# Gate and up products of a two-layer encoder: rounded tokens and their rests side by side as one 512-column product, halves added on GpSimd

## What is computed

```python
h = rmsnorm(x, norm_ffn)
ff = jax.nn.silu(h @ w_gate) * (h @ w_up)
return x + ff @ w_down
```

## Time and profile before

| | |
|---|---|
| median of 3 runs | 1264.53 us (1263.86 to 1264.61) |
| the profiled execution | 1263.36 us |
| its span on the core | 1261.6 us, granted TensorE clock 0.999 of full |
| PE | 1236.0 us busy (98% of the span) |
| DVE | 701.7 us (56%) |
| ACT | 683.6 us (54%) |
| POOL | 672.6 us (53%) |
| chain that ended last | PE 86%, DVE 6%, ACT 4%, issue 2%, POOL 1%, DMA 1% |

### The profile page before, as it was taken

The page is one execution under the profiler, slowest core; times in us unless marked ns, Lnnn a source line. Parts: engine busy times, 40 slices in busy tenths (PEclk is TensorE's granted clock), DMA queues, the critical chain, the costliest instruction groups (busy, mean ns, idle before and its releaser), DMA issues.

```text
span 1261.6 us, 23375 instructions
## 1 busy us (share of the span) xinstructions
PE 1236.0 (98%) x9232; PEld 1072.2 (85%) x9232; DVE 701.7 (56%) x1110; ACT 683.6 (54%) x1342; POOL 672.6 (53%) x484
## 2 busy tenths in 40 slices
PE   7999999999999999999999999999999999999997
PEld 6767787879999999888877777788899999998886
DVE  6845576677776777300058465665877767750003
ACT  6756655448665555432256766554576555553233
POOL 3745752557465354666626776338364433346662
PEclk9999999999999999999999999999999999999999
DMA  6211211232222222332222212214122233323232
GB/s 249 84 52 52 68 51 68 73 145 90 101 102 101 101 101 84 118 100 97 89 72 78 68 51 68 69 51 150 51 85 101 101 108 116 113 85 111 91 99 84
DMA packets 31501, 115.99 MB, mean 92 GB/s; under 512 B 3488, under 2 KB 3872, under 8 KB 31008
## 3 DMA queue, kind: packets, MB, share of 16 engines
q1 hardware_dynamic: 31392, 114.49, 26.5%
HBM read 112.37 MB, written 2.10 MB: 91 GB/s over the span
## 4 chain that ended last, share of the span: by engine, by line
PE 86%; DVE 6%; ACT 4%; issue 2%; POOL 1%; DMA 1%; POOLq 0%; SPq 0%; ACTq 0%; DVEq 0%
PE ps L1998 11%; PE ps L2001 10%; PE ps L2000 10%; PE ps L1855 6%; PE ps L1857 6%; PE ps L1877 6%; PE ps L1874 6%; PE ps L1875 6%; PE ps L1856 6%; PE ps L2157 2%; PE ps L2143 2%; PE ps L1871 2%; PE ps L1866 2%; PE ps L1868 2%; POOL w_lo L1175 1%
## 5 line engine op out<-in xcount | busy, mean ns | idle before, releaser
L1175 POOL TENSOR_TENSOR w_lo<-w_raw,w_hi 128x1024 fp32r<-128x1024 f32 x108 | 265.2, 2457 | 295.7 <-ACT w_hi L686 238.8
L686 ACT ACTIVATE w_hi<-w_raw 128x1024 fp32r<-128x1024 f32 x108 | 114.0, 1056 | 186.4 <-PE ps L1877 170.8
L1998 PE MATMUL ps<-h_hi,w_hi 128*128 128x256 f32 x672 | 191.0, 284 | 0.0
L2000 PE MATMUL ps<-h_lo,w_hi 128*128 128x256 f32 x672 | 190.1, 283 | 0.0
L2001 PE MATMUL ps<-h_hi,w_lo 128*128 128x256 f32 x672 | 190.1, 283 | 0.0
L1855 PE MATMUL ps<-h_hi,w_hi 128*128 128x512 f32 (+1 forms) x392 | 166.3, 424 | 1.4 <-DVE g L1604 0.7
L1998 PE MATMUL ps<-sum_hi,w_hi 128*128 128x256 f32 x528 | 150.2, 284 | 3.6 <-DVE silu L1406 2.2
L1857 PE MATMUL ps<-h_hi,w_lo 128*128 128x512 f32 (+1 forms) x392 | 152.0, 388 | 0.0
L1856 PE MATMUL ps<-h_lo,w_hi 128*128 128x512 f32 (+1 forms) x392 | 151.2, 386 | 0.0
L2000 PE MATMUL ps<-sum_lo,w_hi 128*128 128x256 f32 x528 | 149.4, 283 | 0.0
L2001 PE MATMUL ps<-sum_hi,w_lo 128*128 128x256 f32 x528 | 149.3, 283 | 0.0
(11 more groups left out here) (277 smaller groups left out, 2823.7 us busy)
## 6 DMA issues: line engine op xcount, KB each, us to landing
w_raw<-in_units SPq DMA_DIRECT2D x110, 512.0 KB, 3.5
u<-in_pairs SPq DMA_DIRECT2D x44, 512.0 KB, 4.3
w_raw<-in_pairs SPq DMA_DIRECT2D x40, 512.0 KB, 4.3
gain<-in_gain SPq DMA_DIRECT2D x5, 512.0 KB, 4.3
par<-in_par SPq DMA_DIRECT2D x2, 1214.5 KB, 6.2
x<-in_x SPq DMA_DIRECT2D x4, 512.0 KB, 7.1
spec<-in_pairs SPq DMA_DIRECT2D x4, 512.0 KB, 5.1
out_y<-x SPq DMA_DIRECT2D x3, 512.0 KB, 2.6
```

What stands on the lines that cost most here:

```text
L686: nc.scalar.activation(w_tile(g, 0), w_raw[:, g % RAW], ACT.Copy).then_inc(s_hi, 1)
L1175: nc.gpsimd.tensor_tensor(w_tile(g, 1), w_raw[:, g % RAW], w_tile(g, 0).bitcast(F32), ALU.subtract).then_inc(s_lo, 1)
L1998: nc.tensor.matmul(out, hi[:, cols], factor[m][0][:, k], start=start and k == 0, stop=False, skip_group_check=True)
L2000: nc.tensor.matmul(out, hi[:, cols], factor[m][1][:, k], start=False, stop=False, skip_group_check=True)
```

## The change

For pairs 4 to 21 (`WIDE` = 4) the two matmuls of `m1`, `m6`, `m7` and `m4` that share the rounded weights become one: the rounded tokens and their rests are stored in one tensor (`h_parts`, `sum_parts`), so that one matmul of 512 columns reads both and writes both halves of the bank. The third matmul (rest of the weights) adds to the first half. The bank then holds two partial sums, so:

- ACT copies 512 columns instead of 256 in `copy_m1`, `copy_u2`, `copy_u3`, and a new `copy_gate` copies the bank after `m4` to SBUF;
- POOL adds the halves of each copy (`fold`, 128x256, in place), four a pair, at places of its order that the excerpt below shows;
- `m2` moves to the spare bank's first half, and the filters' and the net's outputs of the first layer's stage to its second half;
- `silu_second(p)` runs on the folded gate in SBUF, behind `copy_u2(p+1)`, and `hidden_second(p)` after the rest of m4(p+1), with both inputs in SBUF;
- `m6` waits for `copy_m1`, not for `gate_first`;
- the filters' `window_sums` on POOL go: a second set of sine values with one half's sign turned lets the filter matmuls over all 128 rows make sum and difference. POOL keeps one addition to a row (`skip_row`), twice.

```diff
+WIDE = 4
+def wide(m, p):
+    return p >= WIDE and m in ("m1", "m6", "m7", "m4")
...
             def copy_u2(L, p):
                 act.wait_ge(prod_done.sem, prod_done.at(L, NUMBER["m6", p] + 1))
+                if p >= WIDE:
+                    act.wait_ge(up1.sem, up1.at(L, p - 1))
...
+                    nc.scalar.activation(wide_u2(p), both(p), ACT.Copy).then_inc(u2c.sem, 1)
+                    return
...
+            def copy_gate(L, p):
+                act.wait_ge(prod_done.sem, prod_done.at(L, NUMBER["m4", p] + 1))
+                act.wait_ge(hid2d.sem, hid2d.at(L, p - 1))
+                nc.scalar.activation(wide_gate(p), both(p), ACT.Copy).then_inc(g2c.sem, 1)
+
             def silu_second(L, p):
+                if p >= WIDE:
+                    act.wait_ge(g2f.sem, g2f.at(L, p - WIDE + 1))
+                    nc.scalar.activation(wide_gate(p)[:, FIRST], wide_gate(p)[:, FIRST], ACT.Silu).then_inc(silu2.sem, 1)
+                    return
...
                     copy_u2(L, p)
+                    if p - 1 >= WIDE:
+                        silu_second(L, p - 1)
                     hi_item(L, NUMBER["m4", p])
...
-                    silu_second(L, p)
+                    if p >= WIDE:
+                        copy_gate(L, p)
+                    else:
+                        silu_second(L, p)
...
+            def fold(L, p, t, copied, at, done):
+
+                pool.wait_ge(copied.sem, copied.at(L, at))
+                nc.gpsimd.tensor_tensor(t[:, FIRST], t[:, FIRST], t[:, SECOND], ALU.add).then_inc(done.sem, 1)
...
                 for j in range(12, N_ITEMS):
+                    m, p = ITEMS[j]
+                    if m == "m3" and WIDE <= p < LAST:
+                        fold_u2(L, p)
                     if not rest_on_vector(j):
                         lo_item(L, j)
-                    m, p = ITEMS[j]
+                    if m == "m2" and p - 2 >= WIDE:
+                        fold_gate(L, p - 2)
+                    if m == "m3" and WIDE <= p < LAST:
+                        fold_u3(L, p)
+                    if m == "m3" and WIDE <= p + 1 < FT:
+                        fold_m1(L, p + 1)
+                    if m == "m3" and p == LAST - 1:
+                        fold_gate(L, p)
...
+                fold_u2(L, LAST)
                 lo_unit(L * UNITS + U_DOWN)
+                fold_u3(L, LAST)
+                fold_gate(L, LAST)
                 lo_unit(L * UNITS + U_DOWN + 1)
...
             def up_second(L, p):
 
                 v.wait_ge(prod_done.sem, prod_done.at(L, NUMBER["m5", p] + 1))
+                if p >= WIDE:
+                    v.wait_ge(u3f.sem, u3f.at(L, p - WIDE + 1))
+                    to = u3w[p % 2][:, FIRST]
+                    nc.vector.tensor_tensor(to, fourth(p), to, ALU.add).then_inc(up2d.sem, 1)
+                    return
...
                     lo_item(L, NUMBER["m4", p])
+                    if p - 1 >= WIDE:
+                        hidden_second(L, p - 1)
...
                 for k in range(KT // 2):
                     cols = slice(P * k, P * k + P)
-                    nc.tensor.matmul(out, hi[:, cols], factor[m][0][:, k], start=start and k == 0, stop=False,
-                                     skip_group_check=True)
-                    nc.tensor.matmul(out, hi[:, cols], factor[m][1][:, k], start=False, stop=False, skip_group_check=True)
-                    last = nc.tensor.matmul(out, lo[:, cols], factor[m][0][:, k], start=False, stop=k == KT // 2 - 1,
+                    if wide(m, p):
+                        nc.tensor.matmul(both(p).rearrange("p (v t) -> p v t", v=2), hi[:, cols], factor[m][:, :, k],
+                                         start=start and k == 0, stop=False, skip_group_check=True)
+                    else:
+                        nc.tensor.matmul(out, hi[:, cols], factor[m][:, 0, k], start=start and k == 0, stop=False,
+                                         skip_group_check=True)
+                        nc.tensor.matmul(out, hi[:, cols], factor[m][:, 1, k], start=False, stop=False,
+                                         skip_group_check=True)
+                    last = nc.tensor.matmul(out, lo[:, cols], factor[m][:, 0, k], start=False, stop=k == KT // 2 - 1,
                                             skip_group_check=True)
```

More of the change, by code:

```diff
@@ L383, in chain, with both, wide_u2, wide_gate @@
             return ps[:, chain_bank(p), FIRST]
+        def both(p):
+            return ps[:, chain_bank(p), :]
         def direct(p):
-            return ps[:, chain_bank(p), SECOND]
+            return ps[:, chain_bank(p), SECOND] if p < WIDE else ps[:, SPARE, FIRST]
+        def wide_u2(p):
+            return u2w[:, (p + 1) % 2]
+        def wide_gate(p):
+            return spec[:, 4 + p % 2]
         def fourth(p):
@@ L730, in copy_m1 @@
             def copy_m1(L, p):
+                if p >= WIDE:
+                    act.wait_ge(prod_done.sem, prod_done.at(L, NUMBER["m1", p] + 1))
+                    act.wait_ge(gate1.sem, gate1.at(L, max(WIDE, p - 1)))
+                    nc.scalar.activation(m1w[:, p % 2], both(p), ACT.Copy).then_inc(m1c.sem, 1)
+                    return
                 act.wait_ge(prod_done.sem, prod_done.at(L, NUMBER["m2", p] + 1))
@@ L743, in copy_u3 @@
                 act.wait_ge(prod_done.sem, prod_done.at(L, NUMBER["m7", p] + 1))
+                if p >= WIDE:
+                    if p == WIDE:
+                        act.wait_ge(xsd.sem, xsd.at(2 * L + 2, 0))
+                    act.wait_ge(hid2d.sem, hid2d.at(L, p - 1))
+                    nc.scalar.activation(u3w[p % 2], both(p), ACT.Copy).then_inc(u3c.sem, 1)
+                    return
                 if p >= 2:
@@ L1842, in _ @@
                         gate_first(L, p + 1)
-                    hidden_second(L, p)
+                    if p < WIDE:
+                        hidden_second(L, p)
                 up_first(L, FT - 1)
+                hidden_second(L, FT - 1)
                 if L + 1 < DEPTH:
@@ L1912, in net_one @@
                     pe.wait_ge(s_feat, 16)
-                nc.tensor.matmul(ps[0:FFN_HY, net_bank(L, 0), 0:SEQ], par[0:EMB, C_W1:C_W1 + FFN_HY], feat, start=True,
+                nc.tensor.matmul(ps[0:FFN_HY, net_bank(L, 0), SECOND if L else FIRST], par[0:EMB, C_W1:C_W1 + FFN_HY], feat, start=True,
                                  stop=True).then_inc(net.sem, 1)
@@ L1947, in filter_half @@
                 at = C_W3 + o * HY + SEQ * n
-                outs = (ps[:, SPARE, FIRST], ps[:, fourth_bank(p), SECOND])
-                for way in range(2):
-                    rows = slice(FFN_HY * way, FFN_HY * way + FFN_HY)
-                    last = nc.tensor.matmul(outs[way], hid_a[rows, t:SEQ:2], par[rows, at:at + SEQ], start=way == 0,
-                                            stop=True, skip_group_check=True)
+                for out, signed in ((ps[:, SPARE, SECOND], hid_a), (ps[:, fourth_bank(p), SECOND], hid_m)):
+                    last = nc.tensor.matmul(out, signed[:, t:SEQ:2], par[:, at:at + SEQ], start=False, stop=True,
+                                            skip_group_check=True)
                 last.then_inc(abp.sem if n else wayp.sem, 1)
@@ L1967, in product @@
                         pe.wait_ge(flo.sem, flo.at(L, 4))
-                    out, start = direct(p), False
+                    if p == WIDE:
+                        pe.wait_ge(hid2d.sem, hid2d.at(L, 3))
+                    elif p > WIDE:
+                        pe.wait_ge(gate1.sem, gate1.at(L, p))
+                    if L + 1 < DEPTH:
+                        if p in (F_NET1 + 2, F_NET2 + 2):
+                            pe.wait_ge(argd.sem, argd.at(L, 1 + (p == F_NET2 + 2)))
+                        if p - 1 in F_HALVES:
+                            o, t, n = F_HALVES[p - 1]
+                            if n:
+                                pe.wait_ge(abr.sem, abr.at(L + 1, 2 * o + t + 1))
+                            else:
+                                pe.wait_ge(wayr.sem, wayr.at(L, 2 * o + t + 1))
+                    out, start = direct(p), p >= WIDE
                 elif m == "m6":
```

114 lines of the change are left out of this document (76 added, 38 removed).

## The result

The changed kernel takes 1377.62 us (median of four runs, 1376.72 to 1378.98), the kernel before 1264.19 us on the same chip: a ratio of 1.0898, interval 1.0883 to 1.0913. The change costs 113.4 us where 70 were forecast. The sign was right; the time lies 3.6 us above the range.

A forecast was written before the change was run, and what follows sets the result against it. A circle of ACT, POOL and DVE, 11.96 us a pair, would bound instead of PE: 1263.36 + 32.2 (second layer) + 37.3 (first) = 1332.9 us profiled, median 1.2 higher, so 1334 us; range 1308 to 1374.

The forecast's parts named there:

- the circle: Each pair's hand-overs among ACT, POOL and DVE, from one m2 rounding to the next: 11.96 us, longer than PE's 9.86.
- the conflict: DVE's hidden_second and POOL's m3 rest, both on SBUF, exclude each other: +1.1 us in some 32 pairs if POOL starts first.
- The folds: POOL's 128x256 additions of copied halves: 0.74 us each, ends 0.40 and 0.89; gate's, u3's on the circle, m1's has time.
- between the two cases, nearer to the one where DVE goes first: hidden_second starts 0.04 us after POOL's m3 rest, between earlier offsets 0.13 (POOL first) and 0.02 (DVE first); taken as 0.42 us.
- Rival 2: DVE and POOL block each other at hidden_second: +1.1 us in some 32 pairs, 35 us, total 1369; chance 0.24.
- Their two DVE products fit into DVE's wait for fold u3, so the circle stays 11.96: First layer's eight filter pairs, already 10.90 us before, cost 0.82 less extra each: -6.6 us.
- Reductions: POOL's 7.08 us sine-argument reductions delay the gate fold in first-layer pairs 6 and 9: +7.1 and +5.8 us.
- Merges: On PE, 576 merges of two 256-column products into one of 512 save 0.014 us each, 8 us at most.
- The filter matmuls over all rows: In eight first-layer pairs they no longer run beside each other: 0 to 0.7 us each uncovered, nothing under the circle.
- Clock: Sign against the forecast: PE's granted clock falling below 1.00 in the longer waits; no size given.

The follow-up runs named there:

- Runs 3: run 2 with each of the four folds adding 16 columns instead of 256; 1313.0 us.
- 9: run 5 with only the folds of the gate and u3 adding 16 columns instead of 256; 1305.5 us.
- 10: run 5 with only the folds of m1 and u2 adding 16 columns instead of 256; 1332.2 us.
- run 4: The change with WIDE = 22, so all pairs take the old narrow products, without folds or gate copies; 1272.97 us, ratio 1.0072 to the kernel before.
- run 5: run 2 with VectorE's two window products of a filter pair ahead of m6's rest instead of behind it; 1334.4 us.
- run 1: The change plus a one-column memset and a wait on GpSimd ahead of m3's rest in pairs 5 to 21; 1341.4 us.
- 7: The change with windows early, up_second written to PSUM and reordered VectorE, ScalarE and GpSimd work, so no fold lies on the circle; 1266.5 us, ratio 1.0020.
- 8: run 7 with each GpSimd reduction split over two pairs and its sine one pair later on ScalarE; 1260.95 us, ratio 0.9974 to the kernel before.
- run 2: The change with the second silu written to the gate's PSUM bank, so hidden_second reads one operand from PSUM; 1339.9 us.

## Why the prediction was wrong

- **That the circle bounds, and its price: right.** With the conflict gone, the pair is 11.93 us (11.96 forecast), and the second layer costs 237.13 - 204.95 = 32.2 us, as forecast. The folds took 0.74, as taken. Runs 3, 9 and 10 show that the gate's and u3's folds are on it and m1's and u2's are not.
- **The failed step: "between the two cases, nearer to the one where DVE goes first".** The offset was right (0.04 forecast, 0.05 measured), the choice was not. Two observations, POOL first at 0.13 and DVE first at 0.02, can't rank a case at 0.04, and the cheap side was taken as the forecast. Nor are they like cases. In both, another DVE instruction with two SBUF operands was still on record as running when POOL started; at 0.02 it was this one, until 269.81, with POOL's start at 269.71:

```profile
269.12 0.69 DVE L1374 TENSOR_TENSOR spec<-spec 128x512 f32<-128x512 f32 x1
```

Ahead of hidden_second stands m4's rest, which reads PSUM. Nearly every hidden_second fell behind POOL: the median of the 36 is 1.524 us, the shortest 0.415. Rival 2 had mechanism, place and price right: +35 us forecast, 36.2 measured, of which the conflict itself is 33.3. It had 0.24; it should have been level with the forecast at least, and the range should have reached beyond it.
- **The second failed step: "Their two DVE products fit into DVE's wait for fold u3, so the circle stays 11.96".** Filter pairs took 12.52 with the conflict gone. The products did fit into that wait, but the circle did not stay, for the change makes m2 wait for them behind m6's rest (run 4: 0.85 us a pair; run 5: 5.5 us in all). This is nearly all of the 45.1 - 37.3 = 7.8 us by which the first layer is over its forecast in run 1. Seven filter pairs took 0.6 us more than 11.92, 4.2 in all, and the first one 15.11, another 3.2 (hidden_second to hidden_second): there PE stood idle for 3.18 us until the window products, and the granted clock was then 0.50 from 452 to 456. Run 5, with the windows early, removes both, so their shares aren't told apart.
- **Reductions: right.** In run 1 the two pairs at each reduction take 6.9 and 5.8 us more together than two steady ones (20.10 + 10.66 and 18.95 + 10.74, less 2 x 11.92), against 7.1 and 5.8 forecast.
- **Merges: mis-sized, without effect.** 0.014 us was measured in a run of 512-column products; between 256-column ones a merge saves 0.007, 4 us in all. It only shows where PE bounds (7, 8). The filter matmuls over all rows, bounded by 0.7, cost 0.04.
- **Clock.** That it falls in the longer waits was named as a sign against me, but had no price in the sum. It fell, to 0.74 in one window of 20 us. In most pairs this cost nothing, since the circle of the other engines set the pace; where PE came late by it, a pass grew by 0.7 to 1.3 us, 3.8 us in the whole change at most (run 1 above). The window, columns as the earlier trace rows:

```profile
420.00:440.00 20.00, 13.57 (x61) 11.96 (x62) 8.22 (x13) 7.51 (x16) 12.66 (x15) 0.74 0.17 53
```

Put together: 1334 forecast, 36.2 for the conflict and the clock in its wake (the change against run 1), and the 7.4 by which run 1 lies over 1334, nearly all of it behind m2's new wait: 1377.6. The last two are differences of runs, so the sum closes by itself; the passes counted above are what carries it.

## What to carry to other kernels

Count a circle through several engines term by term, as if nothing else ran: it came out to 0.03 us in 12 here, while busy shares of 40 to 70% hid it. Where an edit gives a VectorE instruction a second SBUF operand and GpSimd starts an SBUF instruction within a tenth of a microsecond, price both orders and forecast the dear one unless something fixes the order; one operand in PSUM (run 2), or GpSimd's start moved from 0.05 us ahead to 0.11 behind (run 1), was the remedy. For every wait that a change adds, look up what stands ahead of the awaited instruction on its engine; and hand partial sums to a slower engine only where their results have a whole pair of time.

## What the runs showed of the hardware

- Which engine leads is decided by little: POOL 0.05 ahead wins (the change, 30 times), DVE 0.11 ahead wins (run 1), and in the trace of before DVE won with POOL recorded 0.02 ahead, though there a like DVE instruction was already running. The loser waits out the other: DVE +1.1 us behind a 1.3 us rest, POOL +0.17 behind a 0.42 us product. An added 0.1 us instruction saved 36 us.
- GpSimd's two-input addition in place takes 0.22 us for 16 columns and 0.74 for 256; an estimate from the two is 0.19 fixed and 0.0022 a column (runs 3 and the change).
- After PE had stood idle for 2.77 us, its granted clock was 0.50 for 6 us, and the pass took 13.93 us instead of 13.04 (the change, 1128 to 1134).
- A 512-column product among 256-column ones takes 0.236 us to the next start (run 8, mean of 176), against 0.226 in a run of its own kind.
